# Router logits taken from scaled residual rows inside the output projection

## The reference

```python
x = x + gt1[:, None, :] * out                  # out = mixer @ w_o, the output projection
h = rms_norm(x, norm_ffn_g) * (1 + sc2) + sh2  # adaLN: scale and shift per sequence
grp_logits = h @ moe_w_grp + moe_b_grp         # 4 groups
exp_logits = h @ moe_w_exp + moe_b_exp         # 16 experts
# argmax group, two best experts in it, softmax weights
# out += weight * (silu(h @ w_gate) * (h @ w_up)) @ w_down, for the two experts of a token
```

## Time and profile before

| | us |
|---|---|
| median of 3 runs | 2031.12 |
| lowest to highest | 2028.49 to 2037.64 |
| profiled execution | 2039.51 |
| its span | 2037.7 |
| TensorE busy in the span | 1845.2 (91%) |
| VectorE, ScalarE, GpSimd busy | 697.1, 494.9, 99.0 |

### The profile page before, as it was taken

One profiled execution on the slowest core, in us unless ns is written; L12 is line 12 of the kernel. 1 busy time (PEld: TensorE's weight loads), 2 busy tenths in 40 slices (PEclk: granted clock), 3 DMA queues, 4 the chain that ended last, 5 costly groups with the idle time before them and its releaser, 6 DMA issues.

```text
span 2037.7 us, 53464 instructions
## 1 busy us (share of the span) xinstructions
PE 1845.2 (91%) x23728; PEld 1482.9 (73%) x23728; DVE 697.1 (34%) x1796; ACT 494.9 (24%) x1097; POOL 99.0 (5%) x151
## 2 busy tenths in 40 slices
PE   5999999989998686999997899999999979999993
PEld 3776777777776465898887764687666758888883
DVE  5241135656664225001112500405777242111105
ACT  2112123333332003101111200314777221101002
POOL 2000000011111101000000100000000001000001
PEclk9999999999999887999999899897999989999997
DMA  8422543444455594999999982543000177999964
GB/s 288 108 73 80 181 151 116 131 146 150 147 158 174 179 340 179 345 371 364 382 365 279 279 153 96 178 93 87 2 2 2 53 301 278 373 373 373 370 246 152
DMA packets 184409, 413.52 MB, mean 203 GB/s; under 512 B 51350, under 2 KB 121458, under 8 KB 175698
## 3 DMA queue, kind: packets, MB, share of 16 engines
q1 hardware_dynamic: 165410, 357.93, 53.1%
q0 software_dynamic: 11040, 39.85, 5.6%
q10 hardware_dynamic: 7760, 12.79, 1.8%
HBM read 356.83 MB, written 57.91 MB: 204 GB/s over the span
## 4 chain that ended last, share of the span: by engine, by line
PE 70%; DMA 11%; issue 7%; DVE 5%; ACT 4%; DVEq 2%; SPq 1%; ACTq 0%; POOL 0%
PE bank L1863 9%; PE bank L635 8%; DMA wu<-in_moe_w_up_dram 5%; PE bank L1858 5%; PE bank L1621 5%; PE bank L1876 4%; PE bank L2683 3%; PE bank L1882 3%; PE bank L2732 2%; PE bank L2784 2%; DMA xT<-in_ada_w_dram 2%; PE bank L2821 2%; PE bank L652 2%; PE bank L1958 1%; PE bank L1840 1%
## 5 line engine op out<-in xcount | busy, mean ns | idle before, releaser
L1858 PE MATMUL bank<-wg,xsT 128*32 128x384 f32 x1056 | 122.3, 502 | 15.1 <-DMA wu<-in_moe_w_up_dram 10.4
L1863 PE MATMUL bank<-wg,xsT 128*32 128x128 f32 x1056 | 123.7, 279 | 0.0
L1863 PE MATMUL bank<-wu,xsT 128*32 128x128 f32 x1056 | 118.9, 273 | 0.0
L1876 PE MATMUL bank<-wd,actT 128*32 128x384 f32 x1056 | 117.5, 486 | 1.3 <-ACT actT L2056 1.3
L1882 PE MATMUL bank<-wd,actT 128*32 128x256 f32 (+1 forms) x704 | 118.0, 326 | 0.0
L1858 PE MATMUL bank<-wu,xsT 128*32 128x384 f32 x1056 | 117.4, 486 | 0.0
L1863 PEld LDWEIGHTS bank<-wg,xsT 128*32 128x32 f32 x1056 | 116.3, 113 | 1.0
L1863 PEld LDWEIGHTS bank<-wu,xsT 128*32 128x32 f32 x1056 | 115.3, 110 | 2.4
L635 PE MATMUL bank<-xm,wp 128*128 128x272 f32 x480 | 113.3, 395 | 0.0
L2245 DVE COPY ys<-bank 128x384 f32<-128x384 f32 x32 | 17.8, 558 | 264.1 <-PE bank L1882 264.1
L635 PEld LDWEIGHTS bank<-xm,wp 128*128 128x128 f32 x480 | 90.2, 190 | 20.6 <-issue 2.7
(11 more groups left out here) (596 smaller groups left out, 4196.3 us busy)
## 6 DMA issues: line engine op xcount, KB each, us to landing
wg<-in_moe_w_gate_dram SPq DMA_DIRECT2D x22, 2048.0 KB, 21.0
wu<-in_moe_w_up_dram SPq DMA_DIRECT2D x22, 2048.0 KB, 26.3
wd<-in_moe_w_down_dram SPq DMA_DIRECT2D x22, 2048.0 KB, 24.3
xT<-in_ada_w_dram SPq DMA_DIRECT2D x40, 1024.0 KB, 5.5
w<-in_moe_w_gate_dram SPq DMA_DIRECT2D x10, 2048.0 KB, 21.2
fT<-in_moe_w_up_dram SPq DMA_DIRECT2D x10, 2048.0 KB, 27.2
gall<-in_moe_w_down_dram SPq DMA_DIRECT2D x10, 2048.0 KB, 22.6
wp<-in_rwkv_w_rkv_dram SPq DMA_DIRECT2D x24, 512.0 KB, 3.8
```

The lines of the kernel that those rows point to most:

```text
L1858: mm = pe.matmul(ps[32 * j:32 * j + 32, 0:GW], B.xsT[:, k, 32 * j:32 * j + 32], w[:, k, 0:GW], start=k == 0, stop=k == KT - 1)
L1863: mm = pe.matmul(ps[96:128, q * 128:(q + 1) * 128], B.xsT[:, kk, 32 * q:32 * q + 32], w[:, kk, GW:FF], start=kk == 0, stop=kk == KT - 1)
L1876: mm = pe.matmul(bank[4 + b][32 * j:32 * j + 32, 0:384], act_piece(k, j), w[:, k, b * 384:(b + 1) * 384], start=k == 0, stop=k == 3)
```

## The change

The logits no longer wait for the norm. ScalarE writes, for each m as soon as the residual tile is ready, a second tile xc = xT x gain x (1 + scale); VectorE does so for the sample columns. TensorE makes logits from xc inside the projection: rows 0 to 4 after m = 5, row 5 after m = 6, row 6 after m = 7 and row 7 after that, with the tokens stationary (L1644, out: 128 tokens x 20). Since the norm's root is one number per token, it is applied to the 20 logits afterwards: five products with one column of ones (L732) give the sum of squares per token, ScalarE and VectorE take root and reciprocal of a 128 x 5 tile (rc), and the logits are multiplied by it. The shift's own share of the logits, and the bias, are made apart (pe_shift_logits) and added. For token rows, a turn now begins with a product that adds root x shift (L1891, 512 columns, from shifts, a matrix with the shift on its diagonal), then adds xc turned by a product with the identity (L1893; no longer a transpose), and ScalarE multiplies by rc while it copies. The sample columns get their shift from GpSimd. The ranks move from behind the ten turns to behind the fourth. Square tiles shrink to two, PSUM bank 2 is kept free for the logits, and router weights load before the experts' first weights in layer 0 and before w_o block 6 in layer 1.

```diff
-            sq = B.sq[n // 2]
-        act.activation(sq[:, k], B.xT[:, k], ACT.Square).then_inc(S("norm_sq"), 1)
+            act.activation(B.sq[:, k % 2], B.xT[:, k], ACT.Square).then_inc(S("norm_sq"), 1)
+            act.activation(B.xc[n // 2][:, k, 0:SEQ], B.xT[:, k, 0:SEQ], ACT.Copy, scale=B.coef[:, k, 0:1]).then_inc(S("norm_x"), 1)
+        else:
+            act.activation(B.fT[:, k], B.xT[:, k], ACT.Square).then_inc(S("norm_sq"), 1)
+    if n in (1, 3):
+        act.wait_ge(S("route_mm"), n // 2 * 3 + 2)
+        act.activation(B.rc[:, 0:4], B.bank[2][:, MEANS:MEANS + 4], ACT.Sqrt, bias=B.eps_rms[:, 0:1], scale=1.0 / D)
+        act.activation(B.rc[0:NS, 4:5], B.bank[2][0:NS, MEANS + 4:MEANS + 5], ACT.Sqrt, bias=B.eps_rms[0:NS, 0:1], scale=1.0 / D)\
+           .then_inc(S("norm_rt"), 1)
...
+        pe_logits(pe, B, l, KT - 1)
         pe.wait_ge(S("x_ready"), n)
+        for t, rows in TT:
+            mm = pe.matmul(B.bank[2][0:rows, MEANS + t:MEANS + t + 1], B.rstd[:, cols(t)], B.ones[:, 0:1], start=True, stop=True)
+        mm.then_inc(S("route_mm"), 1)
...
-    B.sq = [B.fT, sb(sq, "sq", [128, KT, T])]
+    B.xc = [B.fT, sb(sq, "xc", [128, KT, T])]
+    B.sq = sb(sq, "sq", [128, 2, T])
...
+    B.shifts = B.wo[0]
+    B.shift_s = w3[:, 1024:1024 + KT * NS].rearrange("p (k n) -> p k n", k=KT)
...
     load(3)
+    load_router(sp, B, io, 0)
     load_gate_up(sp, B, io, 0, 0, 0)
...
+OUT_BANKS = (0, 1, 2, 3, 4, 5, 6, 7, 0, 1, 3, 4, 5, 6, 7, 0)
...
+def pe_logits(pe, B, l, row):
+
+    pe.wait_ge(B.sem("norm_x"), KT * (4 if l else 1) + row + 1)
+    for t in (4, 0, 1, 2, 3):
+        rows = TT[t][1]
+        mm = pe.matmul(B.bank[2][0:rows, LOGITS + t * 20:LOGITS + t * 20 + 20], B.xc[l][:, row, cols(t)], B.wr[:, row, 0:20],
+                       start=False, stop=row == KT - 1 and t == 3)
+    return mm
+
+
+def pe_shift_logits(pe, B, l):
+    S = B.sem
+    shift = mod(B, l, 3)
+    pe.wait_ge(S("out_ev"), 16 * l + 13)
+    for k in range(KT):
+        pe.matmul(B.bank[1][:, 0:20], shift[:, k, 0:1].to_broadcast([128, 128]), B.wr[:, k, 0:20], start=k == 0, stop=k == KT - 1)
+    for k in range(KT):
+        mm = pe.matmul(B.bank[1][0:NS, 32:52], B.shift_s[:, k], B.wr[:, k, 0:20], start=k == 0, stop=k == KT - 1)
+    mm.then_inc(S("route_mm"), 1)
...
-                pe.wait_ge(S("out_ev"), q - 7)
+                pe.wait_ge(S("out_ev"), q - 6)
             for k in range(KT - 1 if q < EARLY else 0, KT):
-                mm = pe.matmul(B.bank[q % 8][:, 0:HALF], w[k], x[:, k, half(h)], start=k == 0, stop=k == KT - 1)
+                mm = pe.matmul(B.bank[out_bank(q)][:, 0:HALF], w[k], x[:, k, half(h)], start=k == 0, stop=k == KT - 1)
             mm.then_inc(S("out_mm"), 1)
-
-
-def add_gated(dve, B, ps, h, gate, m):
+        if m == 5:
+            pe.wait_ge(S("router_loaded"), 64 * (n + 1))
+            pe.wait_ge(S("norm_x"), KT * (4 if n else 1) + 5)
+            pe.matmul(B.bank[2][:, LOGITS:LOGITS + 100], B.ident[:], B.lg[:].rearrange("p t c -> p (t c)"), start=True, stop=False)
+            for row in range(5):
+                pe_logits(pe, B, n, row)
+        if m == 6:
+            pe_logits(pe, B, n, 5)
+            pe_shift_logits(pe, B, n)
+        if m == 7:
+            pe_logits(pe, B, n, 6)
...
+    if h:
+        dve.drain()
+        ins = dve.tensor_tensor(xc[:, m, SEQ:T].rearrange("p (b s) -> p b s", s=DS), dst[:, w:HALF].rearrange("p (b s) -> p b s", s=DS),
+                                B.coef[:, m, 1:NC].unsqueeze(2).to_broadcast([128, DB, DS]), ALU.mult)
+    return ins
...
+        if q % 16 == 12:
+            dve.tensor_copy(B.shift_s.rearrange("p k (b s) -> p k b s", s=DS), shift[:, :, 1:NC].unsqueeze(3).to_broadcast([128, KT, DB, DS]))
+            dve.drain()
+        add_gated(dve, B, B.bank[out_bank(q)], q % 2, gate, q % 16 // 2, B.xc[n]).then_inc(S("out_ev"), 1)
         if q % 16 == 8:
             dve_route_setup(dve, B)
-        if q % 16 >= 5 and q % 2:
+        if q % 16 == 13:
+            dve.tensor_tensor(B.shifts, B.ident[:].unsqueeze(1).to_broadcast([128, KT, 128]), shift[:, :, 0:1].to_broadcast([128, KT, 128]), ALU.mult)
+        if q % 16 >= 4 and q % 2 == 0:
             dve.drain()
             add_square(q % 16 // 2 - 1)
+        if q % 16 == 14:
+            dve.wait_ge(S("route_mm"), 3 * n + 1)
+            dve.tensor_tensor(shift_logits(B)[:, 0], B.bank[1][:, 0:20], B.br[:], ALU.add)
+            dve.tensor_tensor(shift_logits(B)[0:NS, 1], B.bank[1][0:NS, 32:52], B.br[0:NS], ALU.add)
...
+    pool.wait_ge(S("norm_rt"), (3, 8)[l])
+    pool.tensor_tensor(B.shift_s, B.shift_s, B.rstd[:, SEQ:T].unsqueeze(1).to_broadcast([128, KT, NS]), ALU.mult).then_inc(S("pool_made"), 1)
+    pool.wait_ge(S("pool_made"), 3 + 2 * PAIRS + l)
+    pool.tensor_tensor(B.xc[l][:, :, SEQ:T], B.xc[l][:, :, SEQ:T], B.shift_s, ALU.add).then_inc(S("norm_done"), 1)
...
-    sp.wait_ge(S("out_mm"), 16 * (l + 1))
+    if l:
+        sp.wait_ge(S("out_mm"), 32)
+        load_up(sp, B, io, l, 2, 2)
...
-    pe.wait_ge(S("router_loaded"), 64 * (l + 1))
-    pe.wait_ge(S("norm_done"), 2 + 3 * l)
-    for k in range(0, KT, 2):
-        for part, (a, b) in enumerate(ROUTE_PARTS):
-            for odd in range(2):
-                r = 32 * (2 * part + odd)
-                mm = pe.matmul(bank[2][r:r + 32, 0:b - a], B.wr[:, k + odd, :], B.fT[:, k + odd, a:b], start=k == 0, stop=k == KT - 2)
-                if k == KT - 2 and odd:
-                    mm.then_inc(S("route_mm"), 1)
 
     def token_turn(q):
         t, rows = TT[q // 2]
+        ps = bank[(q % 7 + 3) % 8]
         if q >= 7:
             pe.wait_ge(S("h_ev"), 10 * l + q - 6)
+        if q == 8:
+            pe.wait_ge(S("norm_done"), 2 + 3 * l)
+        if q == 0:
+            pe.wait_ge(S("norm_rt"), (3, 8)[l])
+        if t < 4:
+            pe.matmul(ps, B.rstd[:, cols(t)], B.shifts[:, q % 2 * 4:q % 2 * 4 + 4].rearrange("p k n -> p (k n)"), start=True, stop=False)
         for k in range(4):
-            mm = pe.transpose(bank[(q % 7 + 3) % 8][0:rows, k * 128:(k + 1) * 128], B.fT[:, q % 2 * 4 + k, cols(t)], B.ident[:])
+            mm = pe.matmul(ps[0:rows, k * 128:(k + 1) * 128], B.xc[l][:, q % 2 * 4 + k, cols(t)], B.ident[:], start=t == 4, stop=t == 4 or k == 3)
         mm.then_inc(S("h_tr"), 1)
 
-    for q in range(2):
+    for q in range(4):
...
         token_turn(q)
-    pe.wait_ge(S("lgt_ev"), 2 * l + 2)
-    for t, rows in TT:
-        part = 0 if t < 2 else 1
-        at = t * 128 - ROUTE_PARTS[part][0]
-        mm = pe.matmul(bank[2 - part][0:rows, 320 + t * 20:340 + t * 20], B.lgT[hs(part), at:at + rows], B.rsel[hs(part)], start=True, stop=True)
-    mm.then_inc(S("route_mm"), 1)
-    for q in range(2, 10):
-        if q == 6:
-            pe.wait_ge(S("route_step"), 6 * l + 1)
-        token_turn(q)
-
     pe.wait_ge(S("route_step"), 6 * l + 3)
     pe.matmul(bank[2][:, 96:96 + C], B.ones[:], B.upper[:, 0:C], start=True, stop=True)
     pe.matmul(bank[2][:, 0:96], B.upper[:], R["m"][:].rearrange("p t e -> p (t e)"), start=True, stop=False)
@@ -1831,6 +1902,8 @@
         n = 5 - t
         mm = pe.matmul(bank[2][:, 16 * (t + 1):96], B.ones[:], R["m"][:, t:t + 1].to_broadcast([128, n, 16]), start=False, stop=t == 4)
     mm.then_inc(S("route_mm"), 1)
+    for q in range(4, 10):
...
+        act.activation(dst, src, ACT.Copy, scale=B.rc[0:rows, t:t + 1]).then_inc(S("h_ev"), 1)
+
+    if l == 0:
+        act.wait_ge(S("slots_zero"), 32 * ZPARTS)
+    act.wait_ge(S("lgt_ev"), l + 1)
+    for q in range(4):
...
-    dve.wait_ge(S("route_mm"), 4 * l + 1)
-    dve.tensor_copy(B.lgT[hs(0), 0:256], bank[2][hs(0), 0:256]).then_inc(S("lgt_ev"), 1)
-    dve.wait_ge(S("router_loaded"), 64 * (l + 1))
-    dve.wait_ge(S("route_mm"), 4 * l + 3)
-    for h in range(2):
-        tt(B.lg[:, 2 * h:2 * h + 2], bank[2 - h][:, 320 + 40 * h:360 + 40 * h].rearrange("p (t c) -> p t c", t=2),
-           B.br[:].unsqueeze(1).to_broadcast([128, 2, 20]), ALU.add)
-    tt(B.lg[0:NS, 4], bank[1][0:NS, 400:420], B.br[0:NS], ALU.add)
+    dve.wait_ge(S("norm_rt"), ROOT_AT[1 + 2 * l])
+    dve.reciprocal(B.rc, B.rc).then_inc(S("lgt_ev"), 1)
+    dve.drain()
+    logits, sl = bank[2][:, LOGITS:LOGITS + 100].rearrange("p (t c) -> p t c", t=5), shift_logits(B)
+    tt(B.lg[:, 0:4], logits[:, 0:4], B.rc[:, 0:4].unsqueeze(2).to_broadcast([128, 4, 20]), ALU.mult)
+    dve.scalar_tensor_tensor(out=B.lg[0:NS, 4], in0=logits[0:NS, 4], scalar=B.rc[0:NS, 4:5], in1=sl[0:NS, 1], op0=ALU.mult, op1=ALU.add)
+    dve.drain()
+    tt(B.lg[:, 0:4], B.lg[:, 0:4], sl[:, 0:1].to_broadcast([128, 4, 20]), ALU.add)
...
-    act_scale(act, B, 1, mod(B, 0, 3))
...
-    dve_out_proj(dve, B, 0, mod(B, 0, 2))
-    dve_norm(dve, B, 1, 1, "g_ffn0", mod(B, 0, 3), mod(B, 0, 4))
+    dve_out_proj(dve, B, 0, mod(B, 0, 2), "g_ffn0")
...
```

65 lines of the change are left out of this document (33 added, 32 removed).

## The result

The changed kernel takes 2065.42 us (median of 4 executions, 2058.06 to 2069.59), the kernel before 2030.37 beside it: ratio 1.0162, interval 1.0123 to 1.0201, so 35 us slower. Forecast were 2046 us and a range of 2030 to 2060: the sign was right, the size less than half. The profiled execution took 2066.69 us (span 2064.9), the one of before 2039.51: the traces explain 27 of the 35 us. Single executions scatter: over all kernels measured here the profiled one lies between 11.1 us under (no_idle) and 9.1 us above (before) the median that it belongs to.

What follows compares the result with a forecast made beforehand. TensorE, holding 70% of the span, was taken to bound the kernel. Projection +23.6, router weights +2.2, P to gather -8.4 and expert loop -2 gave +15.4 us: 2054.9 profiled, 2046 as median, range 2030 to 2060.

Steps and rivals of the forecast that it cites:

- Projection, thin work and clock: Output projection, each layer: new thin passes 8.5 us plus a clock fall 3.3 us, +11.8 us, between 8.5 and 17.
- The place of the fall: In the projection: clock falls for certain at 52 thin passes behind m = 5, every other time behind m = 6; 3.3 us.
- Router weights in layer 0: Layer 0: four router DMAs ahead of the load TensorE waits for delay its landing, +2.2 us, between 0 and 6.
- P to the gather: From the output projection's end (P) to the first expert slot's gather: sooner by 3.7 and 4.7 us, -8.4 us in all.
- Expert loop: Expert loops, both layers: the earlier scatter may shorten TensorE's waits for expert weights, -2 us, between 0 and -12.6.
- The median: Whole kernel: profiled 2039.5 us lies 8.4 above median 2031.1, so 2054.9 by profile becomes 2046.5.
- rival: Whole kernel: clock holds, 2036 to 2040, chance 0.22; thin passes cheap, 2024, 0.10; expert loop gives more, 2036, 0.12.
- here TensorE's work is cheap and in the projection it is not: From the projection's end to the gather, TensorE is mostly idle at clock 0.50, so work there costs little.

Runs made afterwards that it cites:

- no_idle: The changed kernel without the 22 idle products between the token turns and the gather, in both layers: 2059.81 us, ratio 1.0156 to the kernel before.
- logits_after: The changed kernel with every row of logits and the shift's logits moved behind m = 7, after the projection: 2078.89 us, ratio 1.0212 to the kernel before.
- swapped: The changed kernel with the rows' logits made from 32 router columns as weights and moving tokens, then turned: 2067.99 us, ratio 1.0162 to the kernel before.
- router_late: The changed kernel with layer 0's router loads issued behind w_o's block 4 and the first expert's down load: 2058.07 us, ratio 1.0140.

## Why the prediction was wrong

By profiles it forecast +15.4 us, and +27.2 were there. The mechanisms came out as said in the main, and the sizes did not. Term by term:

- **Projection, thin work and clock: 11.8 a layer.** Nearly right in layer 1, 13.2: thin passes 9.1 us at full clock (52 at 0.107, and 42 in the 3.57 us from 1684.30 to 1687.87) where I had 8.5, and 3.8 of clock where I had 3.3 (the 52 passes took 6.85 us instead of 5.56, block m = 6 10.0 instead of 7.5). The low level lasted 4.9 us into dense work instead of 3.2. The place of the fall and block m = 6 as its victim came out as said. In layer 0 it was 13.8 from the landing of the weights on: TensorE had stood 12 us and ran the first products of m = 4 at the lower level (17.07 us for two blocks).
- **Router weights in layer 0: 2.2, range 0 to 6.** Mis-sized: the weights landed 4.6 us later against the first product in these two profiles; by the means over all profiles the wait at m = 4 grew by 3.7 (above). The four issues took 7.73 us instead of the 2.86 of the earlier trace rows. I had seen that the queue was full and still took a value near the quiet one, though the trace of before holds the same four issues on the full queue of layer 0, and there they took 10.0 us (746.61 to 756.61, below). The two layers' projections together: 31.6 against 25.8 forecast, half of the miss.
- **P to the gather: -8.4.** The mechanism was right, turns of 1.75 us (1.73 said) in TensorE's queue, with routing long done; the size was -4.7. The turns began 1.2 and 1.6 us later than said, behind ScalarE's copy of row 7 (TensorE waited 1.33 us for it) and its root (0.95), and in layer 0 their first three groups took 2.08, 1.71 and 1.71 us, where 0.9 is the time at full clock.
- **Expert loop: -2.** TensorE's waits for up weights, over both layers, went from 12.7 to 10.5 us, right in sign; but 6.1 were added in layer 0 and 8.3 vanished in layer 1. The loops as a whole grew by 1.8. A wait of 2.3 us for instructions in layer 1, which the kernel before does not have, takes back what the weights gave; the rest is not traced.
- **The median.** I had subtracted 8.4 us from both sides, as if the changed kernel's profiled execution would lie above its median too. It lies 1.3 above; those of the kernel before lie 9, 8 and 7 us above the medians of their batches. What these 8 us are stays open. In the third batch the profiles of the two kernels are 37.4 us apart (2041.8 and 2079.2), 11.7 of it in the gathers.

The issues on SP's queue in the kernel before, layer 0; the first row is the first of the four, the second is what follows the last of them:

```profile
746.61 3.69 SPq L1744 DMA_DIRECT2D wr<-in_moe_w_grp_dram  x1
...
756.61 0.43 SPq L1726 DMA_DIRECT2D wu<-in_moe_w_up_dram  x1
```

So the failed step is the sum, in three of its terms, and no single one of them carries the miss: the projections with the router's loads (31.6 us measured, 25.8 forecast), the gain behind P (4.7 and not 8.4) and the loop (+1.8 and not -2). On top comes the step from the profile to the median, 8 us that no trace shows. No rival describes it better. One premise does not hold once the change is made: "here TensorE's work is cheap and in the projection it is not". In the changed kernel TensorE's queue sets the gather, and logits_after shows that a thin pass behind P then costs 0.19 us against 0.107. What made the new work dear was its form, tokens as weights: 1.08 us a row, against 0.28 in swapped.

## What to carry over

Price a thin fp32 product by its weight columns, not by what moves (up to 128 columns made no difference here): put the narrow operand on the weight side, even if the result must be turned. Thin work is best put where TensorE already waits for another engine, in groups short enough that dense work keeps the clock. And when a step shortens an engine's idle time, look at the fillers that were hidden in it: here 22 idle products became 5 us of every layer's critical path.

## What was not expected of the hardware

- The clock fell within uninterrupted work: at 32 to 52 thin passes without a gap (0.52, 0.50), though not at each such stretch, and was full again 4.0 and 4.9 us into dense work in the changed kernel.
- On a full queue an issue itself takes microseconds. The router's loads took 6.87, 5.64 and 3.57 us in router_late, against 0.59 to 3.22 in the changed kernel. That does not come from their tiny packets alone: the expert's 2 MB down load just ahead of them took 10.67 us, and 9.07 in the kernel before.
- TensorE stands without instructions for up to 1.5 us at a time in a straight run of products, 11 to 14 us behind the start of a scatter that keeps the DMA engines at 0.9 to 1.06 (6 to 14 us where the scatter starts behind the gather). Waits of up to 3.3 us for instructions also stand in the expert loops, some 250 to 310 us behind a scatter, in most profiles but not in the first two of the kernel before; what brings them about is not shown.
